# Expert up products with the weights held in the array for entries of more than 128 tokens

## What is computed

```python
def body(y, xs_b):
    rt, rw, e = xs_b
    xb = h_pad[rt]
    hid = jax.nn.silu(xb @ w1[e]) * (xb @ w3[e])      # 1024 -> 256, twice: the up products
    ob = (hid @ w2[e]) * rw[:, None]                  # 256 -> 1024: the down products
    return y.at[rt].add(ob.astype(y.dtype)), None
```

## Time and profile before

| | us |
|---|---|
| median of three runs | 2463.86 (2462.97 to 2463.9) |
| the profiled execution | 2483.54 |
| its span, first to last instruction | 2481.8 |
| expert stage in it, from the first L1474 to the last L1547 | about 1584 to 2463 |

### The profile page before, as it was taken

One profiled execution on the slowest core, in us unless ns is written; L12 is line 12 of the kernel. 1 busy time (PEld: TensorE's weight loads), 2 busy tenths in 40 slices (PEclk: granted clock), 3 DMA queues, 4 the chain that ended last, 5 costly groups with the idle time before them and its releaser, 6 DMA issues.

```text
span 2481.8 us, 32549 instructions
## 1 busy us (share of the span) xinstructions
PE 2401.2 (97%) x8544; PEld 1174.5 (47%) x8545; DVE 1182.6 (48%) x2744; ACT 482.6 (19%) x892; POOL 640.1 (26%) x653
## 2 busy tenths in 40 slices
PE   6999999999999999999999999999999999999996
PEld 3444444555544556566444554444444444444442
DVE  3376222666655666666244766433333333343332
ACT  3311000444431133332211121200000000000000
POOL 0000000000021100000211235555454545455551
PEclk9999999999999999999999999999999999999998
DMA  8231334342373133221444214589899999999995
GB/s 259 50 71 44 81 72 128 110 134 92 123 191 80 52 81 94 94 72 61 132 132 125 95 43 179 180 291 295 280 302 332 317 317 335 312 364 344 326 335 126
DMA packets 122933, 437.49 MB, mean 176 GB/s; under 512 B 22205, under 2 KB 24461, under 8 KB 97121
## 3 DMA queue, kind: packets, MB, share of 16 engines
q1 hardware_dynamic: 78208, 306.91, 35.9%
q0 software_dynamic: 44640, 129.49, 19.8%
HBM read 369.72 MB, written 73.93 MB: 179 GB/s over the span
## 4 chain that ended last, share of the span: by engine, by line
PE 84%; DVE 7%; another core or an unknown queue 4%; issue 2%; DMA 1%; ACT 1%; SPq 1%; POOL 0%; DVEq 0%; ACTq 0%; POOLq 0%
PE psum L992 21%; PE psum L1474 17%; PE psum L1077 8%; PE psum L1541 8%; PE psum L1323 7%; PE psum L1340 3%; PE psum L1479 3%; PE psum L1280 2%; PE psum L1547 2%; PE psum L1384 2%; PE psum L1148 2%; PE psum L1158 2%; PE psum L1167 1%; PE psum L1407 1%
## 5 line engine op out<-in xcount | busy, mean ns | idle before, releaser
L992 PE MATMUL psum<-mem 128*128 128x512 f32 x1536 | 689.7, 594 | 1.0 <-DMA mem<-in_w_in 0.8
L1474 PE MATMUL psum<-mem 128*128 x1008 | 449.9, 594 | 1.7 <-DVE mem L2685 1.2
L992 PEld LDWEIGHTS psum<-mem 128*128 128x128 f32 x1536 | 279.2, 191 | 293.6 <-issue 290.5
L785 POOL DMA_INDIRECT mem<-h_d,idx x312 | 316.4, 1014 | 360.3 <-DVE idx L2766 255.4
L1474 PEld LDWEIGHTS psum<-mem 128*128 128x128 f32 x1008 | 186.4, 190 | 230.0 <-issue 230.0
L2744 DVE TENSOR_TENSOR mem<-mem,psum 128x256 f32<-128x256 f32 x93 | 39.1, 421 | 457.2 <-ACT mem L1953 344.0
L1541 PE MATMUL psum<-mem 128*128 128x512 f32 x504 | 229.8, 603 | 15.0 <-ACT mem L1956 13.6
L1077 PE MATMUL psum<-mem 128*128 128x512 f32 x448 | 192.8, 592 | 0.0
L790 POOL DMA_INDIRECT out_x<-mem,put x93 | 142.1, 1527 | 90.5 <-issue 72.3
L1323 PE MATMUL psum<-mem 128*128 128x512 f32 x384 | 165.0, 592 | 0.0
L1541 PEld LDWEIGHTS psum<-mem 128*128 128x128 f32 x504 | 93.4, 191 | 141.0 <-issue 141.0
(11 more groups left out here) (421 smaller groups left out, 2483.1 us busy)
## 6 DMA issues: line engine op xcount, KB each, us to landing
mem<-in_exp_w SPq DMA_DIRECT2D x201, 1024.0 KB
mem<-in_w_in SPq DMA_DIRECT2D x16, 2048.0 KB, 14.4
proj_d<-mem SPq DMA_DIRECT2D x104, 256.0 KB, 2.0
mem<-in_ada_w POOLq DMA_DIRECT2D x16, 1024.0 KB, 6.2
mem<-proj_d POOLq DMA_DIRECT2D x56, 256.0 KB, 3.0
mem<-proj_d POOLq DMA_DIRECT2D x20, 512.0 KB, 5.7
mem<-in_ada_w SPq DMA_DIRECT2D x4, 2048.0 KB, 23.2
mem<-in_w_branch SPq DMA_DIRECT2D x3, 2048.0 KB, 8.2
```

The lines of the kernel that those rows point to most:

```text
L785: g.indirect_dma_start(x[:, 2 * P * n:2 * P * (n + 1)], None, h2_q, bass.IndirectOffsetOnAxis(ap=idx[:, p, j, n:n + 1], axis=0), bounds_ch ...
L992: mm = t.matmul(bank(unit_bank(u)), l, r, start=(k == 0), stop=(k == KD - 1))
L1474: return t.matmul(bank(up_banks[j][r]), xgT[r][:, k, P * j:P * (j + 1)], up_piece(h, r, k), start=(k == 0), stop=(k == KD - 1))
```

## The change

For wide entries the operands of the up product change places. In `up_wide` a 128 x 128 piece of w1 (z = 0) or w3 (z = 1), every second column (f = 0 or 1), is stationary and the tokens are streamed, 160, 192, 224 or 256 columns, whichever is the least that holds n (`by_width`). The result comes out as hidden features by tokens, which is what the down product takes, so DVE's multiplication writes straight into `hidT`; transposes, their copies on ACT and the waits on `e_hT` and `e_hc` are left for entries of up to 128 tokens. Half f = 0 lies in the bank of the first tile, f = 1 in bank 5. `up_wide_begin` does 15 of the 32 products ahead of `turn_hidden`, `up_wide_end` the other 17 after it. The weight buffer of `up_wide` is a constant of the code, so each of the four widths stands twice, for h = 0 and 1.

```diff
-        hid = [view(24064 + 256 * j, FF) for j in range(2)]
+        hid = view(24064, FF)
...
-            def up(j, h, r, k):
-                return t.matmul(bank(up_banks[j][r]), xgT[r][:, k, P * j:P * (j + 1)], up_piece(h, r, k), start=(k == 0), stop=(k == KD - 1))
-
-            def up_half(j, b, k):
+            def up(h, r, k):
+                return t.matmul(bank(up_banks[0][r]), xgT[r][:, k, 0:P], up_piece(h, r, k), start=(k == 0), stop=(k == KD - 1))
+
...
+            def up_wide(b, f, z, k, n):
+                w = w13[b][:, z, k, :].rearrange("p (n f) -> p f n", f=FK)[:, f, :]
+                return t.matmul(psum[:, up_banks[f][b % 2], 2 * P * z:2 * P * z + n], w, xgT[b % 2][:, k, 0:n],
+                                start=(k == 0), stop=(k == KD - 1))
...
-            def up_half_second(b):
+            def up_wide_begin(b, n):
                 for k in range(KD):
-                    mm = up_half(1, b, k)
+                    up_wide(b, 0, 0, k, n)
+                for k in range(KD - 1):
+                    up_wide(b, 0, 1, k, n)
+
+            def up_wide_end(b, n):
+                up_wide(b, 0, 1, KD - 1, n).then_inc(e_H[0], 1)
+                for z in range(2):
+                    for k in range(KD):
+                        mm = up_wide(b, 1, z, k, n)
                 mm.then_inc(e_H[1], 1)
 
+            def by_width(n, part, b):
+
+                with pe.If(n > P + HALF):
+                    with pe.If(n > P + HALF + 32):
+                        part(b, 2 * P)
+                    with pe.Else():
+                        part(b, P + HALF + 32)
+                    pe.nop()
+                with pe.Else():
+                    with pe.If(n > P + 32):
+                        part(b, P + HALF)
+                    with pe.Else():
+                        part(b, P + 32)
+                    pe.nop()
+                pe.nop()
+
             def up_begin(n, h, r):
 
                 with pe.If(n > HALF):
-                    for k in range(UP_AHEAD):
-                        up(0, h, r, k)
+                    with pe.If(n > P):
+                        with pe.If(h > 0):
+                            by_width(n, up_wide_begin, 2 + r)
+                        with pe.Else():
+                            by_width(n, up_wide_begin, r)
+                        pe.nop()
+                    with pe.Else():
...
+                            up(h, r, k)
...
+                    with pe.If(n > P):
+                        seconds.up()
+                        with pe.If(h > 0):
+                            by_width(n, up_wide_end, 2 + r)
+                        with pe.Else():
+                            by_width(n, up_wide_end, r)
+                        pe.nop()
+                    with pe.Else():
+                        for k in range(UP_AHEAD, KD):
+                            mm = up(h, r, k)
+                        mm.then_inc(e_H[0], 1)
+                    pe.nop()
...
-            def up_second(n, h, r):
-
-                seconds.up()
-                with pe.If(n > P + HALF):
-                    for k in range(KD):
-                        mm = up(1, h, r, k)
-                    mm.then_inc(e_H[1], 1)
-                with pe.Else():
-                    with pe.If(h > 0):
-                        up_half_second(2 + r)
-                    with pe.Else():
-                        up_half_second(r)
-                    pe.nop()
-                pe.nop()
...
-                outs.wait(e_hc[1])
...
-                pe.wait_ge(e_hc[0], now)
...
+                    with pe.Else():
+                        turned.wait(e_hc)
...
-            def turn_tile(j):
+            def turn_tile():
                 for f in range(FK):
-                    mm = t.transpose(psum[:, 1, (FK * j + f) * P:(FK * j + f + 1) * P], hid[j].rearrange("t (p f) -> t f p", f=FK)[:, f, :], ident[:, :])
-                mm.then_inc(e_hT[j], 1)
-
-            def turn_half_tile(j):
-                t.transpose(psum[:, 1, FK * j * P:(FK * j + 1) * P], hid[j][:, 0:P], ident[:, :]).then_inc(e_hT[j], 1)
+                    mm = t.transpose(psum[:, 1, f * P:(f + 1) * P], hid.rearrange("t (p f) -> t f p", f=FK)[:, f, :], ident[:, :])
+                mm.then_inc(e_hT, 1)
+
+            def turn_half_tile():
+                t.transpose(psum[:, 1, 0:P], hid[:, 0:P], ident[:, :]).then_inc(e_hT, 1)
...
             def turn_hidden(n, now):
                 with pe.If(n > HALF):
                     with pe.If(n > P):
                         seconds.wait(e_hid[1])
-                        turn_tile(0)
-                        with pe.If(n > P + HALF):
-                            turn_tile(1)
-                        with pe.Else():
-                            turn_half_tile(1)
-                        pe.nop()
                     with pe.Else():
+                        turned.up()
                         pe.wait_ge(e_hid[0], now)
-                        turn_tile(0)
+                        turn_tile()
                     pe.nop()
                 with pe.Else():
+                    turned.up()
                     pe.wait_ge(e_hid[0], now)
-                    turn_half_tile(0)
+                    turn_half_tile()
...
-                    with pe.If(n > P):
-                        up_second(n, h, r)
-                    pe.nop()
...
-                with act.If(n > HALF):
-                    with act.If(n > P):
-                        wide.wait(e_hT[1])
-                        hidden_turned(0, q % 2, P)
-                        with act.If(n > P + HALF):
-                            hidden_turned(1, q % 2, P)
-                        with act.Else():
-                            hidden_turned(1, q % 2, HALF)
-                        act.nop()
+                with act.If(n <= P):
+                    narrow.up()
+                    with act.If(n > HALF):
+                        narrow.wait(e_hT)
+                        hidden_turned(q % 2, P)
                     with act.Else():
-                        act.wait_ge(e_hT[0], now)
-                        hidden_turned(0, q % 2, P)
+                        narrow.wait(e_hT)
+                        hidden_turned(q % 2, HALF)
...
-            def hidden(j, p):
-                v.tensor_tensor(hid[j], sg[:, j, :], bank(up_banks[j][p])[:, FF:2 * FF], ALU.mult).then_inc(e_hid[j], 1)
+            def hidden(dst, j, p):
...
             def hidden_rows(n, now, p):
-                dve.wait_ge(e_si[0], now)
-                hidden(0, p)
                 with dve.If(n > P):
+                    dve.wait_ge(e_si[0], now)
+                    hidden(hidT[p][:, 0, :], 0, p)
                     wide.up()
                     wide.wait(e_si[1])
-                    hidden(1, p)
+                    hidden(hidT[p][:, 1, :], 1, p)
+                with dve.Else():
+                    dve.wait_ge(e_si[0], now)
+                    hidden(hid, 0, p)
```

More of the change, by code:

```diff
@@ L342, in layer_kernel @@
         e_xg = [two("xg0"), two("xg1")]
-        e_H, e_si, e_hid, e_hT, e_hc, e_O, e_ob = (two(n) for n in ("H", "si", "hid", "hT", "hc", "O", "ob"))
+        e_H, e_si, e_hid, e_O, e_ob = (two(n) for n in ("H", "si", "hid", "O", "ob"))
+        e_hT, e_hc = sem("e_hT"), sem("e_hc")
         e_w += [sem(f"e_w{b}") for b in (2, 3)]
@@ L1462, in _ @@
             pe.wait_ge(e_clear, 1)
-            for x in (*e_H, *e_hT, *e_O):
+            for x in (*e_H, e_hT, *e_O):
                 pe.sem_inc(x, 1)
-            seconds, outs = Count(pe, "seconds"), Count(pe, "outs")
+            seconds, outs, turned = Count(pe, "seconds"), Count(pe, "outs"), Count(pe, "turned")
             n_now, n_last = pe.alloc_register("n_now"), pe.alloc_register("n_last")
@@ L1477, in up_half @@
                 w = w13[b][:, :, k, :].rearrange("p w (n f) -> p f w n", f=FK)
                 for f in range(FK):
-                    mm = t.matmul(psum[HALF * f:HALF * (f + 1), up_banks[j][b % 2], :].rearrange("p (w n) -> p w n", w=2)[:, :, 0:P],
-                                  xgT[b % 2][:, k, P * j:P * j + HALF], w[:, f, :, :], start=(k == 0), stop=(k == KD - 1))
-                return mm
+                    mm = t.matmul(psum[HALF * f:HALF * (f + 1), up_banks[0][b % 2], :].rearrange("p (w n) -> p w n", w=2)[:, :, 0:P],
+                                  xgT[b % 2][:, k, 0:HALF], w[:, f, :, :], start=(k == 0), stop=(k == KD - 1))
@@ L1497, in up_begin @@
             def up_begin(n, h, r):
                 with pe.If(n > HALF):
-                    for k in range(UP_AHEAD):
-                        up(0, h, r, k)
+                    with pe.If(n > P):
[5 more added lines that the diff above has]
+                    with pe.Else():
+                        for k in range(UP_AHEAD):
+                            up(h, r, k)
@@ L1512, in up_end @@
                 with pe.If(n > HALF):
-                    for k in range(UP_AHEAD, KD):
-                        mm = up(0, h, r, k)
-                    mm.then_inc(e_H[0], 1)
```

(11 more changed lines are left out.)

11 lines of the change are left out of this document (5 added, 6 removed).

## The result

| | median | lowest to highest |
|---|---|---|
| kernel before | 2463.87 us | 2462.97 to 2463.9 |
| changed kernel | 3339.51 us | 3335.87 to 3346.53 |

The ratio is 1.3557, with a 95% interval of 1.354 to 1.3573. The change makes the kernel slower by 876 us. The forecast had the sign, and the cause, but put the size at 206 us; the time lies far outside its range. The profiled execution has a span of 3334.7 us.

What follows compares the result with a forecast made beforehand. PE's array was taken to bound the kernel (busy 2401 of 2482 us), transfers close behind. 2463.9 - 35 (products 20, transposes 15) + 241 for instruction supply gave 2670 us; range 2418 to 2850 us.

Steps and rivals of the forecast that it cites:

- Products: Wide entries' up products on PE: 296.9 us instead of 316.7, a gain of 20 us.
- Both bounds for the strided load: Weights read at every second column: 0.165 us a pass loses 9 us; 0.22 us a pass makes 366 us.
- Transposes and copies: 26 entries above 128 tokens lose three or four transposes on PE: a gain of 15 us.
- The waits for ACT: PE's waits for ACT's copies ahead of the down products would go: counted at 0, bound 12 us.
- Transfers: Rival: code kept, but DMA transfers take back 12 of the 35 us gained: 2441 us, chance 0.07.
- load-bound: Rival: the strided weight load sets the pace at 0.22 us a pass on PE: 2498 us, chance 0.05.
- next to nothing: Rival: code not kept, but stalls are under three per entry and end under the lead: about 2464 us, chance 0.04.
- the code is kept: Rival: the loop's code stays in PE's instruction memory and the array's full saving shows: 2429 us, chance 0.24.
- Whether the code is kept: PE's loop body grows from 936 to 2,680 instructions, above 2048: not kept and exposed, +241 us, chance 0.60.
- Stalls per entry: 3.5 branches per entry on PE's sequencer find their code gone, 9.2 us of standing sequencer per entry.
- Their length: Each branch that finds its code gone lasts 2.64 us, the mean of two (2.07 and 3.21).
- What the lead hides: PE's sequencer lead hides 5.6 us per entry, 3.6 exposed over 67 entries: +241 us; ends +41 and +612.

Runs made afterwards that it cites:

- two widths, moved by 102: Changed kernel with only widths 192 and 256, its loop shifted 102 instructions by a never-run block ahead of it: 2450.87 us, ratio 0.9952 to the kernel before.
- kernel with one width: Changed kernel with every entry above 128 tokens streaming 256, three of four code copies gone: 2487.6 us, ratio 1.0091 to the kernel before.
- 1,624: Changed kernel cut to the widths 192 and 256, loop not moved: 2962.09 us, ratio 1.197 to the kernel before.
- 1,964: Kernel before with 256 never-run instructions ahead of the begin and of the end block of each item: 3079.21 us.
- dead code in two places: Kernel before, work unchanged, with 384 never-run products and loads ahead of the begin and of the end block of each item: 3172.06 us.

## Why the prediction was right and wrong

**Products: right.** Foreseen were 0.134, 0.161, 0.188 and 0.215 us a pass for 160, 192, 224 and 256 columns; the medians from start to start are 0.136, 0.163, 0.189 and 0.216. The kernel with two widths, moved by 102, shows it at 192 (5.53/34 = 0.163):

```profile
2212.51 5.08 PE psum L1486 x30
2217.59 0.23 PE psum L1605 x2
2217.82 5.53 PE psum L1486 x34
```

Both bounds for the strided load fall (0.165 added up, 0.22 flat), for a pass of 160 columns takes 0.136. The Trainium skill ("SBUF — State Buffer", on SBUF cachelines), has it that a read with at least two hits in a 16-byte line keeps its full rate, as two fp32 at a step of two do; this measurement agrees with it as far as the stream's pace lets it be seen. The new loads themselves take 197 ns in the median (kernel with one width), where contiguous ones take 190.

**Transposes and copies: right.** One width costs 26 entries of 64 passes of 0.216, 359.4 us, for 316.7: +43, less the 15 for the transposes +28; measured +23. No run takes the 15 by itself. The waits for ACT had been counted at 0. They are gone from the trace and give little: the profiled run of the kernel before lay 19.7 us over the median, that of one width doesn't (2485.7 us of span, 2487.6 in the median), as if the recording had made those waits; that is not shown.

**Transfers, load-bound, next to nothing: rightly small.** The rival "the code is kept" (2429) had about the right price for its case, as far as an estimate tells, for no run keeps four widths. Two widths kept give 2450.9; four would save 3·64·0.027 + 6·64·0.027 = 16 us more on the array, 2435. So the supply costs the changed kernel, by this estimate, 3339.5 - 2435 = some 904 us. The forecast had 241 for it.

**Whether the code is kept: right answer, wrong rule.** The text took 2,048 instructions as the limit, by the Trainium skill ("Runtime: NRT & Kernel Launch", Instruction fetch mechanics). Loops of 1,624 and 1,964 were lost. Eight packets fit the runs, but as whole packets, with one of them taken by a packet that isn't the loop's, so that seven were left for the loop in every run. That it is the one behind the loop is argued from the one packet more that each lost pass draws; the trace doesn't say which packet comes. The same section says that a branch out of the window of two pages forces a fetch; here five to seven packets stayed, jumps among them included. The change was so large that this didn't matter for it.

**Stalls per entry: right.** 3.5 foreseen; 209 over 67 entries are 3.1.

**Their length: too short.** 2.64 us, the mean of the two in the first pass, against 4.26. The trace shows of what a stall consists. The sequencer goes on about 1.4 us after a packet has landed (nine in ten between 1.34 and 1.54), and a packet takes 0.9 to 2.4 us to come. When it starts varies most: in 35 stalls one starts 1.0 to 1.1 us behind the branch, and these last 3.98 us in the mean. In others the last packet starts late: at 2204.31 us one starts 1.3 us behind the branch and the next 5.5 us behind it, and the branch ends only after that, at 7.8 us. That the first of two is the next in line, asked for ahead of the wanted one, is argued and not shown, since the packets bear no address. Of the 209 stalls 108 saw two packets land, 4.82 us in the mean, and 95 one, 3.82 us. The 2.07 and 3.21 us lie below both: two stalls of a first pass were used as a mean, and were nearer to a lower bound. Now 891/67 = 13.3 us of a standing sequencer per entry, for 9.2.

**What the lead hides: too much.** The forecast hid 5.6 of its 9.2 us per entry under the sequencer's lead, which left 3.6. The idle time of PE grew by 670.7 - 23 = 647 us, 9.7 per entry, so of 13.3 only 3.6 are hidden. The lead was read where the sequencer runs freely; a likely reason is that with three stalls an entry each begins before the lead of the last is won back. The upper end of that term, 9.1 us per entry, was nearly it.

**The clock: not in the sum.** The stage's granted clock is 0.75 to 0.81 in stretches of 200 us, two of which stand above, where it was 1.00: of its 1746 us 750 pass at 1.2 GHz. Of the array's busy time 442 us fall at that level; at 2.4 they would be half, so it costs 221 us. Two steps of the chain show it, a run of 16 passes of 512 columns (some 6.9 us at full clock) and one of 34 of 256 (7.35):

```profile
2058.36 8.67 PE psum L1573 x16
2102.72 9.14 PE psum L1486 x34
```

The clock falls behind stretches in which the array had stood. In the stage of the kernel before it had done so once, for 3.4 us at 1619, and the forecast gave it no term. The 221 is worked out; no run changes the clock alone. The busy time of the stage bears it out (the kernel before, with dead code in two places, the changed one):

```profile
1584.00:2463.00 879.00, 855.89 (x2868) 380.93 (x2868) 314.94 (x650) 72.61 (x198) 448.81 (x396) 1.00 0.93 308
1584.00:3165.00 1581.00, 1051.60 (x2870) 443.75 (x2868) 319.28 (x652) 73.40 (x199) 450.32 (x397) 0.82 0.56 176
1584.00:3330.00 1746.00, 1066.41 (x3401) 624.18 (x3401) 315.14 (x649) 55.44 (x143) 450.33 (x397) 0.79 0.51 160
```

The same products take 856 us in the first and 1052 in the second, 196 more, of which half of the 368 us at the lower clock makes 184.

Together: 647 + 221 - 35 = 833 us, of 867 by which the stage has grown. The dead code in two places, with nothing gained, makes the same sum without the 35: 529 us of idle time, 23 of it there before, and the 184 of the clock: 506 + 184 = 690, for 702 measured in the stage. So the failed step is the size of the supply term, which had 241 us for some 904, by three factors: the length of a stall (13.3 us of a standing sequencer per entry for 9.2), the cover (3.6 us for 5.6), and the clock (221 us for none).

## What to carry to other kernels

Before code in a loop is multiplied by cases, count the instructions of the body on that engine, and the packets of 256 in which it lies with its place in the program: here seven stayed, and at eight nearly every pass drew all of them again, for 1.6 to 2.1 us of time per packet. A size just below the cliff may need nothing but a shift (two widths: 2958 or 2451 us, the same loop), and rarely run code belongs in one place instead of beside each use (5 us or 708 here). If instructions are missing on the array's engine, price the whole chain: the packet ahead of the wanted one, a lead that isn't won back in time, and the lower clock behind each gap.

## What the runs showed of the hardware that was not expected

- A loop in 8 packets draws 9 in every pass (in 25 of 33 where only its last few instructions lie in the eighth), one in 7 draws none: the cliff is one packet wide, and 40 instructions of place are worth 365 us. Whether the oldest packet is dropped or the one that was not used for longest isn't told apart: in a loop that is walked in one direction both lose all.
- What is held isn't one stretch of code: a loop of 2,473 instructions with six packets' worth of dead code in one place ran within 5 us of one with 936.
- In the kernel before, the first pass costs time too, and the kernel with two widths waits there for instructions for 8.7 us, where that with one width waits for 3.0. These 5.7 us would be most of the difference between its 2450.9 and the 2443 foreseen; no run shows it.
- Chips differ more than the smaller effects: the kernel before took 2462.9 to 2465.0 us in most comparisons, and 2477.2 and 2484.6 on two other chips. Each ratio here compares kernels on the same chip.
